# Hybrid decoder step: half of the softmax normalisation on VectorE, key bias made in the sparse stage, loads spread between stores

## The reference, cut to what matters

```python
def stick_breaking(q, k, v, q_pos, k_pos):                    # 6 heads x 64
    z = einsum('bqhd,bkhd->bhqk', q, k) * HEAD_DIM ** -0.5
    causal = k_pos[None, :] < q_pos[:, None]
    log_keep = where(causal, log_sigmoid(-z), 0.0)
    after = cumsum(log_keep, axis=3, reverse=True) - log_keep
    a = where(causal, exp(log_sigmoid(z) + after), 0.0)
    return einsum('bhqk,bkhd->bqhd', a, v)

def dsa_attend(q, qi, wi, q_pos, k, v, ki, k_pos, topk):      # 6 query heads, 2 kv heads
    score = ...                                               # indexer
    _, idx = top_k(score, topk)                               # 256 keys per query
    logits = einsum(q, k[idx]) * HEAD_DIM ** -0.5
    p = softmax(where(valid, logits, -inf))
    return einsum(p, v[idx])
```

## Time and profile before

| | us |
|---|---|
| median of 3 runs | 4918.51 |
| lowest and highest | 4911.43 and 4924.42 |
| profiled execution | 4918.52 |
| its span, first to last instruction | 4916.8 |

### The profile page before, as it was taken

The page is one execution under the profiler, slowest core; times in us unless marked ns, Lnnn a source line. Parts: engine busy times, 40 slices in busy tenths (PEclk is TensorE's granted clock), DMA queues, the critical chain, the costliest instruction groups (busy, mean ns, idle before and its releaser), DMA issues.

```text
span 4916.8 us, 70636 instructions
## 1 busy us (share of the span) xinstructions
PE 4611.4 (94%) x25102; PEld 2611.4 (53%) x25102; DVE 3545.4 (72%) x5925; ACT 1621.7 (33%) x2392; POOL 1346.7 (27%) x1329
## 2 busy tenths in 40 slices
PE   6987999999999999899989889999998999989999
PEld 4433545744466666564454334457444766665643
DVE  1675999999888653454426869999998896535544
ACT  2552101100266676330025521011003666753300
POOL 3220145300111598110032101363001117971100
PEclk9999999999999999999999999999999999999999
DMA  2102111211321002786211021112114110028832
GB/s 68 37 13 64 59 23 32 74 50 49 116 75 53 25 21 80 247 267 190 98 45 34 17 67 54 22 33 76 49 49 133 53 55 23 27 88 281 270 124 86
DMA packets 343697, 396.41 MB, mean 81 GB/s; under 512 B 100279, under 2 KB 264210, under 8 KB 340018
## 3 DMA queue, kind: packets, MB, share of 16 engines
q1 hardware_dynamic: 318002, 375.10, 24.4%
q10 hardware_dynamic: 25344, 16.79, 1.2%
HBM read 297.71 MB, written 94.14 MB: 80 GB/s over the span
## 4 chain that ended last, share of the span: by engine, by line
PE 81%; DVE 5%; SPq 4%; DMA 3%; issue 3%; ACT 2%; POOL 2%; ACTq 0%; POOLq 0%; DVEq 0%
PE banks L838 19%; PE banks L841 14%; PE banks L1975 10%; PE banks L314 5%; PE banks L1389 4%; PE banks L1378 4%; PE banks L1134 4%; PE banks L349 3%; PE banks L1149 3%; PE banks L1405 3%; PE banks L1115 3%; DVE arena L439 3%; PE banks L1693 2%; DMA arena<-in_cache_dsa_kv 2%; SPq L1077 1%
## 5 line engine op out<-in xcount | busy, mean ns | idle before, releaser
L940 DVE TENSOR_SCALAR_CACHE_REDUCE arena<-arena 128x384 uint8<-128x384 f32 (+14 forms) x960 | 1405.2, 1533 | 6.9 <-DVE arena L978 0.5
L838 PE MATMUL banks<-arena 128*128 128x512 f32 x2176 | 937.4, 592 | 0.0
L841 PE MATMUL banks<-arena 128*128 128x384 f32 (+3 forms) x2336 | 720.3, 464 | 3.0 <-POOLq L144 3.0
L838 PEld LDWEIGHTS banks<-arena 128*128 128x128 f32 x2176 | 409.9, 189 | 523.2 <-issue 523.2
L1452 POOL TENSOR_SCALAR arena<-arena 128x128 f32<-128x128 f32 (+15 forms) x192 | 578.4, 3026 | 62.2 <-DVE arena L1478 59.3
L1253 DVE TENSOR_TENSOR_SCAN arena<-arena 128x129 f32<-128x129 f32 (+3 forms) x480 | 508.3, 1111 | 73.9 <-ACT arena L1173 60.5
L841 PEld LDWEIGHTS banks<-arena 128*128 128x128 f32 (+1 forms) x2336 | 417.5, 182 | 269.3 <-issue 62.9
L439 DVE SCALAR_TENSOR_TENSOR arena<-arena 128x512 f32<-128x512 f32 (+3 forms) x532 | 404.3, 760 | 119.6 <-ACT arena L409 70.0
L1975 PE MATMUL banks<-arena 128*128 128x512 f32 (+1 forms) x1088 | 472.5, 597 | 13.6 <-DMA arena<-in_w_out 13.6
L1467 DVE CUSTOM_DVE_ANT_0 arena<-banks,arena 128x512 f32<-128x512 f32 (+3 forms) x480 | 269.7, 607 | 236.9 <-PE banks L1378 236.7
L349 PE MATMUL banks<-arena 64*128 64x512 f32 (+3 forms) x1216 | 306.0, 588 | 59.4 <-ACT arena L409 58.1
(11 more groups left out here) (189 smaller groups left out, 5485.0 us busy)
## 6 DMA issues: line engine op xcount, KB each, us to landing
arena<-in_cache_sb_kv SPq DMA_DIRECT2D x256, 384.0 KB, 4.3
arena<-in_cache_dsa_kv SPq DMA_DIRECT2D x144, 128.0 KB, 4.2
arena<-in_x_prompt SPq DMA_DIRECT2D x32, 512.0 KB, 4.5
arena<-mixT SPq DMA_DIRECT2D x32, 512.0 KB, 4.1
arena<-xs SPq DMA_DIRECT2D x32, 512.0 KB, 4.4
arena<-in_cache_dsa_kv ACTq DMA_DIRECT2D x112, 128.0 KB, 4.7
arena<-in_w_in SPq DMA_DIRECT2D x8, 1536.0 KB, 7.6
out<-arena SPq DMA_DIRECT2D x64, 192.0 KB, 1.9
```

Source lines behind the costliest of these rows:

```text
L838: m = nc.tensor.matmul(bank[i % 4][:, :], W2[c % 2][:, k, j * P:(j + 1) * P], xT[:, k, t * FREE:(t + 1) * FREE], start=(k == 0), stop=(k = ...
L841: m = nc.tensor.matmul(bank[i % 4][0:rows_of(t), 0:WD[name]], xT[:, k, t * P:t * P + rows_of(t)], W2[c % 2][:, k, 0:WD[name]], start=(k == ...
L940: nc.vector.tensor_scalar(out[0:r, 0:v.shape[-1]], v, thr[0:r, t:t + 1], 0.0, ALU.is_ge, ALU.add, accum_out=cnt[0:r, t:t + 1]).then_inc(s_ ...
```

## The change

- In `sparse_gpsimd` only head 0 is multiplied by the inverted sum; head 1 is multiplied by VectorE right behind the inversion, with a semaphore of its own (`s_dn1`), for which the transposes wait as well.
- `bias_end` of tiles 2 to 15 moves from `stick_vector` to `sparse_vector`: that of tile t + 1 at the head of turn (t, 2), in front of that job's additions.
- In `stick_sync` the 48 bias stores are spread, six behind each of the y stores 0 to 7; the loads of pair 1 stand behind stores 0, 1 and 2, those of pair 2 behind 3, 4 and 5, those of the sparse stage behind 7 and 8.
- The maximum's two steps share one semaphore.

```diff
@@ stick_sync
-            for b in range(NB):
+
+            def store_bias(b):
                 a = 32 * (b // 2) + b % 2
                 for h in range(HDSA):
                     r = (b * HDSA + h) * NQ
                     sp.dma_start(SBD[r:r + NQ, :], scs[a:a + 2 * NQ - 1:2, :]).then_inc(s_bs, 16)
-            load_stick_qk(sp, l, 1)
-            load_stick_values(sp, l, 1, 0, NT, s_bvl[1])
-            load_gate(1)
+
             for g in range(4 * NPAIR):
                 p, q = g // 4, g % 4
                 sp.wait_ge(s_by, at(s_by, l * 48 + 4 * (g + 1)))
                 sp.dma_start(YTD[256 + p * P:256 + (p + 1) * P, q * FREE:(q + 1) * FREE], byo[g % 2]).then_inc(s_bys[g % 2], 16)
+                if g < NB:
+                    store_bias(g)
+                if g == 0:
+                    load_stick_qk(sp, l, 1)
+                if g == 1:
+                    load_stick_values(sp, l, 1, 0, NT, s_bvl[1])
+                if g == 2:
+                    load_gate(1)
                 if g == 3:
                     sp.wait_ge(s_bv, at(s_bv, l * NSU + SPAIR))
                     load_stick_qk(sp, l, 2)
+                if g == 4:
                     load_stick_values(sp, l, 2, 0, NT, s_bvl[0])
+                if g == 5:
                     load_gate(2)
                 if g == 7:
                     sp.wait_ge(s_bv, at(s_bv, l * NSU + 2 * SPAIR))
                     load_sparse_keys(sp, l)
                     load_sparse_queries(sp, l, 0)
+                if g == 8:
                     load_sparse_values(sp, l)
                     load_sparse_queries(sp, l, 1)
@@ stick_vector
             for n in range(NSU + GL):
-                if n % 8 == 4 and n // 8 < NSEL - 1:
-                    bias_end(SELTILES[n // 8])
@@ sparse_tensor, transposes
-                pe.wait_ge(s_dn, at(s_dn, 2 * (J0 + f + 1)))
+                pe.wait_ge(s_dn, at(s_dn, J0 + f + 1))
+                pe.wait_ge(s_dn1, at(s_dn1, J0 + f + 1))
@@ sparse_gpsimd
-                for g in range(2):
-                    nc.gpsimd.tensor_scalar(lg[e % 4][:, g, 0:w], lg[e % 4][:, g, 0:w], ri[e % 4][:, g:g + 1], None, ALU.mult).then_inc(s_dn, 1)
+                nc.gpsimd.tensor_scalar(lg[e % 4][:, 0, 0:w], lg[e % 4][:, 0, 0:w], ri[e % 4][:, 0:1], None, ALU.mult).then_inc(s_dn, 1)
@@ sparse_vector
                 if e < NDJ:
                     t, c = DJOBS[e]
+                    if c == 2 and t + 1 in SELTILES[0:NSEL - 1]:
+                        bias_end(t + 1)
+                    if c == 0 and t >= SELTILES[0]:
+                        dve.wait_ge(s_bias, at(s_bias, l * NSEL + t))
                     if e >= 4:
                         dve.wait_ge(s_dt, at(s_dt, U0 + DFIRST[e - 3]))
...
                     nc.vector.reciprocal(ri[r % 4], rs[r % 4]).then_inc(s_dr, 1)
+                    w = (DJOBS[r][0] + 1) * P
+                    dve.wait_ge(s_dr, at(s_dr, J0 + r + 1))
+                    nc.vector.tensor_scalar(lg[r % 4][:, 1, 0:w], lg[r % 4][:, 1, 0:w], ri[r % 4][:, 1:2], None, ALU.mult).then_inc(s_dn1, 1)
```

More of the change, by code:

```diff
@@ L1291, in build @@
         s_dz, s_db = sem("logits_in_psum"), sem("logits_biased", 4)
-        s_dm, s_dx, s_de = sem("maximum_ready"), sem("minus_maximum_ready", 2), sem("exp_logits_ready", 8)
-        s_dr, s_dn = sem("sum_inverted", 4), sem("p_normalised", 8)
+        s_dx, s_de = sem("minus_maximum_steps", 4), sem("exp_logits_ready", 8)
+        s_dr, s_dn, s_dn1 = sem("sum_inverted", 4), sem("p_normalised", 4), sem("p_normalised_second", 4)
         s_dt, s_dc, s_dav = sem("p_transposed", 4), sem("pT_ready", 1), sem("pT_applied", 2)
@@ L1421, in exps @@
                 w = (DJOBS[e][0] + 1) * P
-                act.wait_ge(s_dx, at(s_dx, J0 + e + 1))
+                act.wait_ge(s_dx, at(s_dx, 2 * (J0 + e + 1)))
                 nc.scalar.activation(lg[e % 4][:, g, 0:w], lg[e % 4][:, g, 0:w], ACT.Exp, bias=nm[e % 2][:, g:g + 1],
@@ L1470, in sparse_vector @@
                     dve.wait_ge(s_db, at(s_db, 2 * (U0 + DFIRST[e + 1])))
-                    nc.vector.reduce_max(nm[e % 2], mx[e % 2][:, :, 0:x + 1], AX_X).then_inc(s_dm, 1)
-                    dve.wait_ge(s_dm, at(s_dm, J0 + e + 1))
+                    nc.vector.reduce_max(nm[e % 2], mx[e % 2][:, :, 0:x + 1], AX_X).then_inc(s_dx, 1)
+                    dve.wait_ge(s_dx, at(s_dx, 2 * (J0 + e) + 1))
                     nc.vector.tensor_scalar(nm[e % 2], nm[e % 2], -1.0, None, ALU.mult).then_inc(s_dx, 1)
@@ L1476, in sparse_vector @@
                     dve.wait_ge(s_de, at(s_de, 2 * (J0 + r + 1)))
-                    dve.wait_ge(s_dn, at(s_dn, 2 * (J0 + r - 3)))
+                    dve.wait_ge(s_dn, at(s_dn, J0 + r - 3))
                     nc.vector.reciprocal(ri[r % 4], rs[r % 4]).then_inc(s_dr, 1)
+                    w = (DJOBS[r][0] + 1) * P
+                    dve.wait_ge(s_dr, at(s_dr, J0 + r + 1))
+                    nc.vector.tensor_scalar(lg[r % 4][:, 1, 0:w], lg[r % 4][:, 1, 0:w], ri[r % 4][:, 1:2], None, ALU.mult).then_inc(s_dn1, 1)
                 for f in DGATES[e]:
```

## The result

The changed kernel takes 4954.6 us (median of 4 runs, 4949.49 to 4961.48) against 4917.4 us before (4 runs, 4911.43 to 4924.42). The ratio is 1.0077 with a 95% interval of 1.006 to 1.0094: slower by 37 us. The profiled execution took 4961.48 us, its span is 4959.7. The new kernel's lines stand eight to ten lower: GpSimd's multiplication is L1460, VectorE's L1493, the bias L1240, the logit additions L1479, the gates L1270 and L1500, the transposes L1398, the value products L1414, the logits L1386.

A forecast was written before the change was run, and what follows sets the result against it. TensorE, busy 94% of the span, was taken as the bound, with no hole in the sparse stage's body. The sum was 4918.5 - 22.5 - 3.2 - 6 - 14.2 + 39 + 9 + 15 = 4935.6, so 4936 us, range 4875 to 4968.

The forecast's parts named there:

- a wait at tiles 1 to 7: Sparse stage: the moved bias costs 0 to 8.8 us per layer at these tiles; half taken, 9 us lost.
- Stick stall: Stick stage: issuing y stores earlier removes the gate's wait and the low clock behind it in both layers, 22.5 us gained.
- Bias edits: Stick stage: fourteen key-bias operations leave VectorE, 1.6 us per layer, 3.2 us gained (bounds 1 to 6).
- tempting 4 us per collision: Stick stage: booking 4 us per bias meeting GpSimd's difference was rejected; each yields only its own time, 0.5 and 0.8 us.
- Start of the sparse stage: Sparse stage's start, where GpSimd was said to pace the small jobs: splitting the normalisation gives 6 us gained (0 to 14).
- Holes at tiles 8 to 14: Sparse stage: bias waits out GpSimd's multiplication and delays TensorE's logits, 19.5 us per layer, 39 us lost.
- Clock behind the holes: Sparse stage: TensorE holes of 4 to 4.5 us lower the clock, some 7.5 us per layer, 15 lost (0 to 25).
- End: Sparse stage's end: one GpSimd multiplication instead of two, 4.8 us plus 2.3 of clock per layer, 14.2 us gained.
- Why the bias blocks: Sparse stage, third jobs: bias behind reciprocal, normalisation and gate, GpSimd just begun, so it waits out nearly the whole GpSimd operation.
- Rival (a): Sparse stage: the bias doesn't block TensorE, only the gains stand, 4873 us; chance 0.20.
- takes the shared path late: Sparse stage: GpSimd seems to claim the shared path late, so VectorE's multiplication goes first and GpSimd ends about 0.4 us later.

The follow-up runs named there:

- b1: The kernel before with only SyncE's new order of stores and loads in the stick stage: 4894.23 us, ratio 0.9962.
- a1: The changed kernel with the fourteen bias instructions back at their old places in the stick stage: 4892.75 us, ratio 0.9964.
- b3: The kernel before with only the bias instructions moved into the sparse stage, GpSimd still multiplying both heads: 4912.85 us, ratio 0.9998.
- b2: The kernel before with only the split of the normalisation (head 0 GpSimd, head 1 VectorE): 4916.4 us, ratio 1.0005.
- c3: The changed kernel with VectorE multiplying the second head only in the last tile's three jobs, GpSimd both heads elsewhere: 4881.21 us, ratio 0.9932.
- a2: The changed kernel with the bias after the third job's negative maximum, in front of the reciprocal, instead of at the job's head: 4895.24 us, ratio 0.9956.
- c1: The changed kernel with the bias back in the stick stage and VectorE's multiplication behind the gates in all but the last four turns: 5019.28 us, ratio 1.0209.
- a4: The changed kernel with GpSimd multiplying only half of head 0's columns, the rest left unnormalised (results not right): 4889.54 us in a single run.
- c2: The changed kernel with GpSimd's multiplication of more than 1024 columns cut into two instructions, same work: 4899.06 us, ratio 0.9975.

## Why the prediction was right, and where it wasn't

Predicted were 4936 us in a range of 4875 to 4968, slower as the likeliest side; measured 4954.6. The deciding mechanism, a bias that waits for GpSimd and holds TensorE's logits back, is there, at the tiles named. That the total came within 19 us is in part luck: a gain at the start that was a loss (17 us) and a clock priced too low stood against a wait at tiles 1 to 7 that hardly came (7 us). Step by step, both layers, from the stages of the two traces:

| | forecast | measured |
|---|---|---|
| stick stage (stall 22.5, bias 3.2) | -25.7 | -26.2 |
| sparse, tiles 0 to 7 (start -6, bias +9) | +3 | +10.9 |
| sparse, tiles 8 to 14 (holes 39, clock 15) | +54 | +68.7 |
| sparse, last tile | -14.2 | -13.2 |
| sum | +17.1 | +40.1 |

- **Stick stall: right.** The stores alone give 4894.2 us, and their stick stages are 11.8 and 11.9 us shorter, 23.7 for 22.5. Nothing came late behind it.
- **Bias edits: not resolved.** The changed kernel's stick stages are 0.5 and 2.0 us shorter than those of the stores alone, 2.5 for 3.2. But `b1` and `a1` have the same stick stage, and in layer 1 it takes 326.6 and 328.3 us, so the 2.5 is not clear of the spread; the same edit in `b3` shows 6.8. The tempting 4 us per collision isn't there: the scan took its place in the queue (6.37 us for two beside GpSimd's 5.44), as the prediction had it from the earlier trace rows. The Trainium skill (SBUF — State Buffer, Who interferes with whom) says that a VectorE instruction with two SBUF inputs contends with a GpSimd instruction that reads SBUF, and the trace agrees.
- **Start of the sparse stage: the step that failed.** "At the start, where GpSimd paces the small jobs" was read from a stretch in which GpSimd was at 18.3 of 20 us and TensorE idle 2.5. Now GpSimd is at 9.4 there and TensorE idle 2.3. What I left out is that the gate stands behind VectorE's multiplication and TensorE's value products wait for the gate: 7.4 us in `a1`, 2.6 in `b1` without a split, 1.6 with the multiplication behind the gate. GpSimd's load and TensorE's holes stood in the same stretch, but nothing showed one as the cause of the other; the source of the hole was not looked up. From `b1` to `a1` the split loses 5.3 and 5.6 us by tile 8, where I had 3 gained per layer: 11 lost for 6 gained. The bias at tiles 1 to 7, from `a1` to the changed kernel, costs 1.2 and 0.9 us where I had 4.4 per layer. The other -2 of the table's +10.9 is the longer half-clock stretch with which the kernel before opens layer 0.
- **Holes at tiles 8 to 14: right.** 4.4 was forecast for tile 14 and 4.73 measured; 18.5 per layer for the five holes (2.8 at tile 8, where its own terms give 3.0) against 19.5, and 1.0 for tiles 9 and 11 against some 2. The addition at tile 14 stands 7.2 us behind the reciprocal instead of 0.16, a move of 7.1 where the sum had 6.6, since GpSimd took 6.15 us and not 5.12, partly made up by the gate, which ran beside it; 2.4 us of it were hidden, where 2.2 were counted.
- **Clock behind the holes: undersized, and wrongly summed.** The prediction's own terms, three losses of 2.3 us and two of half that, make 9.2 per layer, not the 7.5 that it booked. Measured are about 10.7: 2.1 us for each hole, 1.7 for each of the two of 2.9 us in layer 0, where halving had given 1.15. It adds up: tiles 8 to 14 lost 34.3 us per layer, and holes (19.5), clock (10.7), tiles 9 and 11 (some 2) and the split alone in tile 8 (1.3) leave under 1.
- **End: right.** 5.35 us of waiting became 1.03, and the clock stays up, which is worth 6.6 us per layer for 7.1. In `b2` (layer 0) and `c3` it doesn't quite: 3.4 us at half clock cost 1.6.
- **Why the bias blocks: half right.** The text had the bias "directly behind the reciprocal, normalisation and gate", with GpSimd "just begun". Which of these matters it didn't say, and my expectation for `b3`, where the normalisation isn't there, shows that I took it for harmless: 55 to 80 us were expected and nothing came. It is the 1.2 us of normalisation that put the bias behind GpSimd. Rival (a)'s condition, "if GpSimd claims it later than the normalisation and gate last", was the right question. Its price was 20 us too low: in `a1` and `a2`, at 4893 and 4895, the bias doesn't block, and 4873 was forecast; the split's start, 11 us lost where 6 were booked as gained, is most of it.
- **GpSimd "takes the shared path late": wrong as a reading of the earlier trace rows.** Its two cases differ in moment (0.83 and 1.67 us into GpSimd's instruction) and in size (512 and 1152 columns), and the text took the moment. The changed kernel decides for the size: 0.82 us behind the start of 1024 columns the bias gets through, 0.87 behind that of 1152 it is held. For that reason tiles 1 to 7 were nearly free. All that is left of the late claim is 0.08 us, in `b3`, and `c1` speaks against even that.

What stays open: why an instruction of GpSimd over 1024 columns holds VectorE's plain multiply to its end and a narrower one doesn't. The changed kernel and `c1` show the border between 1024 and 1152, `a4` and `c2` agree with it; none looks inside. Nor is it settled why at 0.08 us behind GpSimd a bias goes first (`b3`) and a multiplication doesn't (`c1`): the one has constants as operands, the other a multiplier from memory, and they work on different buffers. The 10.7 us per layer of the clock are half of TensorE's busy time at 0.50; no run has the same holes at full clock, and the check is tile 8, whose two layers differ in that stretch alone.

## What to carry to other kernels

Before work is moved from an engine that is busy but not bounding to VectorE, list what stands behind the new instruction in VectorE's queue and who waits for it; here that price ate the whole gain, and only at the stage's end, where TensorE truly waited for GpSimd, did the split pay. Two edits that share an engine have to be tried together and apart: bias and split cost nothing alone and some 60 us together, because one lined the other up behind a GpSimd instruction. Where a stall has one known place, change the kernel at that place alone.

## What the runs showed of the hardware

- A plain VectorE `tensor_scalar` in f32 (1.2 us at 2048 columns) issued in the middle of a GpSimd `tensor_scalar` of over 1024 columns waits for its end: 5.95 us behind 1920 columns, 3.63 behind 1152. Beside 1024 columns or fewer it is slowed but not held: 1.47 us at 1152 columns, 0.75 when GpSimd is idle; 1.89 at 2048, 1.22 when GpSimd is idle. Issued 0.06 us before GpSimd's start it goes first, and GpSimd is longer by 1.03 us (6.15 for 5.12).
- Issued 0.08 us behind GpSimd's start, a bias still goes first (1.22 us) and a multiplication doesn't (5.67 us, `c1`). The starts in the records don't tell which engine has the path.
- The form with the accumulator doesn't wait: 2.27 us inside GpSimd's 6.16.
- A scan with two inputs in SBUF takes 5.25 us beside one GpSimd subtraction of 2048 columns, 2.2 beside pieces of 512, and 1.2 free.
- Behind TensorE holes of 2.9 us, as behind those of 4.2 to 4.7, the granted clock was 0.50 for a stretch (1.2 GHz); the cost was about half of TensorE's busy time in it, 1.6 to 3.3 us behind the holes of 2.9.
